# RMS norm of a hybrid decoder step: squared tiles summed on GpSimd, one matmul with ones per norm

## The reference

```
def rmsnorm(x, g, eps=1e-6):
    y = x * lax.rsqrt(jnp.mean(x * x, axis=-1, keepdims=True) + eps)
    return y * g

for i in range(2):
    h = rmsnorm(x, norm_mix[i]);  cp = h @ w_in[i]
    ya, yb, yc = rwkv7(cp...), retention(cp...), mamba2(cp...)
    x = x + concatenate([ya, yb, yc]) @ w_out[i]
    h = rmsnorm(x, norm_ffn[i])
    x = x + (swiglu(h) if i == 0 else moe_swiglu(h))    # top 2 of 8 experts
y = rmsnorm(x, norm_final)
```

## Time and profile before

| | |
|---|---|
| median of three runs | 1709.55 us (1705.39 to 1720.24) |
| the profiled execution, own time | 1713.85 us |
| its span, first to last instruction | 1712.0 us |
| TensorE busy with matmuls | 1522.5 us, 89% of the span, 10644 entries |
| VectorE busy | 926.5 us, 54% |
| ScalarE busy | 741.5 us, 43% |
| GpSimd busy | 110.8 us, 6%, 144 instructions |
| mean granted TensorE clock | 0.853 |

### The profile page before, as it was taken

One profiled execution on the slowest core, in us unless ns is written; L12 is line 12 of the kernel. 1 busy time (PEld: TensorE's weight loads), 2 busy tenths in 40 slices (PEclk: granted clock), 3 DMA queues, 4 the chain that ended last, 5 costly groups with the idle time before them and its releaser, 6 DMA issues.

```text
span 1712.0 us, 27530 instructions
## 1 busy us (share of the span) xinstructions
PE 1522.5 (89%) x10644; PEld 1298.8 (76%) x10644; DVE 926.5 (54%) x1453; ACT 741.5 (43%) x1108; POOL 110.8 (6%) x144
## 2 busy tenths in 40 slices
PE   4899999895889999888999989684899999999996
PEld 3887778773789999877877777473677787778775
DVE  4623544424444344355156533445298888888885
ACT  4511233212343243362113321133187778777874
POOL 0000110201000000000011011100000000000000
PEclk8967888755889999978689985586599999999998
DMA  7211200101534444332120020050197789878982
GB/s 275 89 36 38 68 26 26 53 15 46 183 118 150 137 147 147 123 96 63 38 69 14 26 78 15 42 187 13 38 349 282 285 295 347 283 286 294 348 279 83
DMA packets 62054, 234.83 MB, mean 137 GB/s; under 512 B 7056, under 2 KB 7152, under 8 KB 61072
## 3 DMA queue, kind: packets, MB, share of 16 engines
q1 hardware_dynamic: 59328, 217.61, 37.0%
q0 software_dynamic: 2496, 13.71, 2.1%
q10 hardware_dynamic: 144, 2.28, 0.3%
HBM read 225.48 MB, written 8.09 MB: 136 GB/s over the span
## 4 chain that ended last, share of the span: by engine, by line
PE 55%; issue 31%; DVE 8%; ACT 4%; POOL 1%; DMA 1%; POOLq 0%; ACTq 0%; DVEq 0%
PE bank L459 11%; PE bank L461 9%; PE bank L460 9%; PE bank L453 8%; PE bank L723 2%; ACT whi L1100 2%; PE bank L570 1%; PE bank L473 1%; PE bank L588 1%; PE bank L858 1%; PE bank L602 1%; DVE wlo L1497 1%; PE bank L600 1%; PE bank L811 1%; DMA x<-in_x 1%
## 5 line engine op out<-in xcount | busy, mean ns | idle before, releaser
L1497 DVE TENSOR_TENSOR wlo<-wraw,whi 128x1024 fp32r<-128x1024 f32 x410 | 500.9, 1225 | 406.2 <-ACT whi L1100 393.7
L1100 ACT ACTIVATE whi<-wraw 128x1024 fp32r<-128x1024 f32 x410 | 433.2, 1060 | 442.4 <-PE bank L461 351.4
L459 PE MATMUL bank<-hh,whi 128*128 128x320 f32 x968 | 343.1, 354 | 57.8 <-DVE hl L1517 36.0
L460 PE MATMUL bank<-hl,whi 128*128 128x320 f32 x968 | 318.2, 329 | 0.0
L461 PE MATMUL bank<-hh,wlo 128*128 128x320 f32 x968 | 317.6, 328 | 0.0
L459 PEld LDWEIGHTS bank<-hh,whi 128*128 128x128 f32 x968 | 197.7, 204 | 81.6 <-issue 49.2
L460 PEld LDWEIGHTS bank<-hl,whi 128*128 128x128 f32 x968 | 199.7, 206 | 1.9 <-issue 1.0
L461 PEld LDWEIGHTS bank<-hh,wlo 128*128 128x128 f32 x968 | 199.3, 206 | 0.0
L1018 PE MATMUL bank<-whi,hh 128*128 128x512 f32 (+1 forms) x384 | 148.9, 388 | 1.1 <-DVE place L2043 1.1
L1020 PE MATMUL bank<-wlo,hh 128*128 128x512 f32 (+1 forms) x384 | 144.2, 375 | 0.0
L1019 PE MATMUL bank<-whi,hl 128*128 128x512 f32 (+1 forms) x384 | 144.1, 375 | 0.0
(11 more groups left out here) (380 smaller groups left out, 2205.6 us busy)
## 6 DMA issues: line engine op xcount, KB each, us to landing
wraw<-in_w SPq DMA_DIRECT2D x410, 512.0 KB, 4.9
smb<-in_s_ssm POOLq DMA_DIRECT2D x2, 1536.0 KB, 7.6
out_o_ssm<-smb POOLq DMA_DIRECT2D x2, 1536.0 KB, 5.6
cst<-in_consts ACTq DMA_DIRECT2D x1, 2225.0 KB, 12.6
srw<-in_s_rwkv POOLq DMA_DIRECT2D x2, 768.0 KB, 6.5
out_o_rwkv<-srw POOLq DMA_DIRECT2D x2, 768.0 KB, 4.5
x<-in_x SPq DMA_DIRECT2D x1, 1280.0 KB, 12.4
out_y<-x SPq DMA_DIRECT2D x1, 1280.0 KB, 4.5
```

Source lines behind the costliest of these rows:

```text
L459: mm(out, hi, rh, start=first, stop=False)
L460: mm(out, hi, rl, start=False, stop=False)
L1100: af(whi[:, ring % HI, :], wraw[:, POS[ring], :], ACT.Copy).then_inc(S("slot_hi"), 1)
L1497: tt(wlo[:, POS[ring], :], wraw[:, POS[ring], :], whi[:, ring % HI, :].bitcast(F32), ALU.subtract).then_inc(S("slot_split"), 1)
```

## The change

The squares are no longer multiplied one by one. GpSimd adds the tiles into one (`sums`, new), in the second `htmp` buffer, and TensorE multiplies the ones with that tile alone. A new semaphore `sq_added` says how many tiles are in the sum; it frees the buffers of squares in place of `sq_used`, and `ms_done` lets ScalarE take the root. The first add counts two tiles; each further add waits for the one before, since it reads what that wrote.

```diff
@@ tensor
-            def norm(i, tiles=range(KT)):
-                for k in tiles:
-                    pe.wait_ge(S("sq_ready"), KT * i + k + 1)
-                    m = mm(B[0][:, 0:T], C("ones"), sqb[:, k % 2, :], start=(k == 0), stop=(k == KT - 1))
-                    m.then_inc(S("sq_used"), 1)
+            def norm(i):
+                pe.wait_ge(S("sq_added"), KT * (i + 1))
+                mm(B[0][:, 0:T], C("ones"), htmp[:, 1, :], start=True, stop=True).then_inc(S("ms_done"), 1)
@@ tensor, output projection
                     full_slot(G_OUT[l] + j, G_OUT[l] + j, B[6 + j % 2][:, 0:T])
-                    if j >= 2:
-                        norm(2 * l + 1, [j - 2])
-                norm(2 * l + 1, range(KT - 2, KT))
+                norm(2 * l + 1)
@@ scalar
-                        act.wait_ge(S("sq_used"), KT * i + k - 1)
+                        act.wait_ge(S("sq_added"), KT * i + k - 1)
                     af(sqb[:, k % 2, :], x[:, k, :], ACT.Square).then_inc(S("sq_ready"), 1)
 
             def norm(i):
-                act.wait_ge(S("sq_used"), KT * (i + 1))
+                act.wait_ge(S("ms_done"), i + 1)
@@ gpsimd
+            def sums(i):
+
+                for k in range(1, KT):
+                    gp.wait_ge(S("sq_ready"), KT * i + k + 1)
+                    if k > 1:
+                        gp.wait_ge(S("sq_added"), KT * i + k)
+                    tt(htmp[:, 1, :], sqb[:, 0, :] if k == 1 else htmp[:, 1, :], sqb[:, k % 2, :], ALU.add)\
+                        .then_inc(S("sq_added"), 2 if k == 1 else 1)
...
             gp.dma_start(par[:, :], par_in[0]).then_inc(S("par_in"), 16)
+            sums(0)
             gp.wait_ge(S("const_in"), 16)
             for l in range(DEPTH):
                 if l:
+                    sums(2 * l)
                     gp.wait_ge(S("h_split"), KT * 2 * l + 1)
...
                 out(p_rw[l], srw_p[:, :, :])
+                sums(2 * l + 1)
...
+            sums(2 * DEPTH)
             gp.wait_ge(S("st_out"), 16 * 6 * DEPTH)
```

## The result

The changed kernel takes 1726.06 us (median of 20 runs, 1712.91 to 1739.0), the kernel before 1713.45 us beside it (20 runs, 1698.93 to 1733.9). The ratio is 1.008, interval 1.005 to 1.011: slower by 0.8%, some 12.6 us. The forecast was 2.5 us slower, 1712 on the median of three runs that stood for before then. With 20 runs that base is 1713.45, so of the 14.1 us between 1712 and 1726.06 some 3.9 are the base, and some 10.1 us are missing in the sum. The profiled execution of the changed kernel took 1716.11 us (span 1714.2, mean granted clock 0.850) against 1713.85 (1712.0, 0.853) of before.

What follows compares the result with a forecast made beforehand. TensorE was taken to set the pace in norms 1 and 3, a dependent chain to bound norms 0, 2 and 4. Terms +0.1 - 1.2 + 3.6 - 1.2 + 1.2 gave +2.5 us: 1712 us, range 1704 to 1722.

Steps and rivals of the forecast that it cites:

- Price of one add: GpSimd's chained adds in the norms: 0.93 us a step, with 0.88 and 1.38 as ends.
- rival 1: GpSimd's chained adds: handover costs 0.5 us, not 0.05, step 1.38; slower by 12 us, 1722; chance 13%.
- Contention: Norms 1 and 3: each GpSimd add waits for VectorE's weight split to end, costing nothing within a 3.5 us slot.
- DVE split durations unchanged at 1.23 us: Sign that the forecast is right: VectorE's weight splits keep their length of 1.23 us.
- Rival 3: Norm 0: last add gets no turn until VectorE's three weight splits end; 4.1 us late, 1716; chance 10%.
- The clock: TensorE's single matmuls after over 4 us of idling run at half clock, 1.47 us; restart after the norm loses nothing.
- Norms 1 and 3: Output projections: 2.70 us gained in slots, 1.5 lost at the end; net -1.2 us each, bounds -1.8 and -0.3.
- Norm 2: Bare chain of squares and adds, with nothing to hide it: loss 3.6 us, bounds 2.7 and 6.3.
- Norm 4: Chain of adds longer, but the root's table load becomes hidden: loss 1.2 us, bounds 0.4 and 3.9.
- Norm 0 and the moved DMAs and memsets: Sum arrives just under the weight splits' cover, loss 0.1 us; DMAs and memsets 7.4 us later cost nothing.
- The sum: All five norms together: +0.1 - 1.2 + 3.6 - 1.2 + 1.2 = +2.5 us, 1712 us on the median.
- The bounds: Whole kernel: 1704 to 1722 us, covering all rivals and the scatter of a median; within 1%: 92%.

Runs made afterwards that it cites:

- e5: Changed kernel with three useless ScalarE copies ahead of the root in norms 1 and 3: 1.0156 of before, mean 1729.9 us.
- e8: The kernel before, unaltered, run once more for a second profile: 1717.62 us.
- e1: The changed kernel again, unaltered: 1.0038 (1.0001 to 1.0075) of before, mean 1727.7 us.
- e2: Kernel before with only norms 1 and 3 summed on GpSimd: 0.9928 (0.9882 to 0.9973) of before, mean 1709.0 us.
- e4: Changed kernel with TensorE also multiplying ones with each squared tile in norms 0, 2 and 4, result overwritten: 1.0064 of before, mean 1726.9 us.
- e6: Kernel before with only norms 1 and 3 on GpSimd, repeated on another chip: 0.9948 (0.9893 to 1.0003) of before, mean 1715.9 us.
- e12: Changed kernel with norm 2 alone back on TensorE: 1.0005 (0.9967 to 1.0044) of before, mean 1717.1 us.
- e14: Kernel before with eight useless copies ahead of the root in norm 2, second group: 1.0049 (1.0013 to 1.0085) of before, mean 1726.4 us.
- e7: Kernel before with eight useless copies ahead of the root in norm 2, first group: 1.0117 (1.0046 to 1.0187) of before, mean 1724.0 us.
- e13: Kernel before with four useless copies ahead of the root in norm 2: 1.0004 (0.9974 to 1.0034) of before, mean 1716.9 us.

## Why the prediction was wrong

The direction (slower by less than 1%) and most of the mechanism of the parts were right, the time was not: 1726.06 lies above the range to 1722. The step that failed is the sum. It puts norm 2's longer chain in at its own length, +3.6 us, and everything outside the norms at nothing. Measured, that chain is +3.94 us, but a bare delay of 3.7 us there costs 7.1 and 9.8 us in the means of two groups, the stages behind norms 1 and 3 give +1.7, and the mixers, which had no term, differ by -18.6 and +16.2 us between the two profiles. A further 3.9 us of the distance to 1726 is the base, a median of three executions: on 1713.45 the same sum gives 1716. Point by point:

- **Price of one add.** Forecast 0.93 us a step, measured 1.00 (0.86 for the add). The high end of 1.38, on which rival 1 rested, does not occur; rival 1 would have given 1722, and what came is as slow for another reason.
- **Contention.** As forecast, the add waits for the weight split in norms 1 and 3 and this costs nothing. The Trainium skill, "SBUF — State Buffer", section "Who interferes with whom", says that the first to take the port keeps it; the trace agrees: 1.54 us for the add beside the split, 0.86 alone. In norm 0 it is the other way about: the last add was first, as forecast, and VectorE's split beside it took 1.47 us, against the sign "DVE split durations unchanged at 1.23 us"; nobody waited for it. Rival 3's 4.1 us did not come.
- **The clock.** "The restart after the norm is at half clock already, so nothing is lost there" fails twice. First, the restart is 0.63 and 0.61 us longer, since TensorE works 5.5 and 6.1 us at half clock before the clock rises, instead of 4.1 and 4.8 (20 and 22 matmuls instead of 14 and 17); and SwiGLU has a second such stretch, +1.5 us, against -1.0 in the experts: together +1.7. By e5 this comes with the time of the return, by e8 the SwiGLU part occurs in before too. Second and larger, the clock's course in the mixers is in no term (see the sum below). The matmul priced at 1.47 us took 1.43 or 0.81: half clock after 4.30 us of idling isn't certain, nor is full. Over the twelve norms 1 and 3 in which GpSimd adds (after, e1, e2, e4, e6, e12) it was slow in three and fast in nine, so its price there was mostly too high.
- **Norms 1 and 3.** -1.14 and -1.76, forecast -1.2 each with -1.8 as the end; right. Slots of 3.52 us, right.
- **Norm 2.** +3.94 for a forecast of +3.6, nearly all from the step of 1.00. Right as a stretch, wrong as a price in the sum. A bare delay of 3.7 us in before gives +7.1 us in the mean of one group (e14, 5 either way) and +9.8 in another (e7, 10 either way); undoing norm 2 alone brings the changed kernel back to 1.0005 (e12).
- **Norm 4.** +1.63, forecast +1.2. With TensorE's matmuls this stretch is 8.6 to 10.2 us over seven profiles (mean 9.3), with GpSimd's adds 10.35 to 10.37 over five: +1.1 against that mean, so the forecast is right and the pair's +1.63 partly chance.
- **Norm 0 and the moved DMAs and memsets.** No reader was late. Of the +0.41, 0.23 us is ScalarE's idling ahead of the table load: the cover ends at a step of 0.96 us, as forecast, and the step was 1.00. The rest is less than before's own scatter: norm 0 takes 11.3 to 12.4 us over nine profiles with TensorE's matmuls, since the squares stand 1.07 us apart for more or less of it before they come closer, and 11.9 to 12.0 over seven with GpSimd's adds.
- **The sum.** Fixed stretches +4.8 for a forecast +2.5; of the 2.3 between, 1.7 is the clock behind the norms, and the rest is the step of 1.00 us and the pair's chance in norms 0 and 4, less what norm 3's fast matmul gave. The remaining 5 to 8 us of the measured 10 to 13 were in no term. That they come in the mixer of layer 1, behind norm 2, is argued from e12 and e14 and not measured: that mixer takes 410.9 to 417.6 us in the seven profiles with the long norm 2, 410.2 in e13, and 401.4 to 414.9 in the five with a short one.
- **The bounds.** The forecast took a measurement's scatter of 15 us for noise around a fixed sum. It is not: in every whole kernel measured the times follow the mean granted clock, by 1.3 to 2.1 us for each 0.001, and an edit can change how often the good courses occur.

What is shown: a delay in norm 2, by its length alone, makes before slower (e14, e7), and without norm 2's longer chain the rest of the change costs nothing measurable (e12). What is not: how a delay of 3.7 us keeps the mixer of layer 1 from its short course (401 us in before, 404 in e12, never under 410 with the delay), whether the same delay at another place would do the same (norms 0 and 4 were not tested alone, and e5 leaves it open for norms 1 and 3), and how large the surcharge is. The bare delay costs 7.8 us over e7 and e14 together, 3 to 12, which still holds its own 3.7. That there is more rests on the changed kernel, 9.1 us over its two groups (6 to 12) with fixed stretches of 4.8, and on the 0 of 79 executions. No run holds the clock's course and keeps the delay.

The best version found is the change in norms 1 and 3 alone: 0.993 (0.988 to 0.997) on one chip, 0.995 (0.989 to 1.000) on another, where its mean was not better. Its fixed stretches promise 1.6 us.

## What to carry to other kernels

Matmuls that add up in PSUM get the sum without an instruction of their own. Replacing them by adds pays only where the adds lie beside other work: a chained add of 128x320 costs 1.00 us a step, the square and matmul it replaces 0.71 at full clock (pairs of squares 1.42 us apart in e7), so a norm that nothing covers is longer by all of the difference. At half clock the old pair takes 1.07 us, and adds lose nothing. Norm 4 of e7, where TensorE does the sums (timeline of ScalarE, then the window over it, columns as above, granted clock 0.50):

```profile
1706.92 0.47 ACT L1117 ACTIVATE sqb<-x 128x320 f32<-128x320 f32 x1 [0.60 <-PE bank L473]
1707.98 0.47 ACT L1117 ACTIVATE sqb<-x 128x320 f32<-128x320 f32 x1 [0.60 <-PE bank L473]
1705.00:1710.00 5.00, 5.00 (x11) 2.96 (x10) 0.00 (x0) 1.88 (x4) 0.00 (x0) 0.50 0.01 3
```

Where a profile has long stages with TensorE between its two clocks, look at their granted clock first; a delay of a few us ahead of such a stage may cost twice its length (3.7 us, e14) or nothing that can be measured (1.87 us, e13). One profiled execution of each kernel can't decide there an edit of 1%: here the pair showed +2.3 us for a loss of 10, and only the distribution of some dozens of executions and an undo of one part did.

## What the runs showed of the hardware

The same program, the same 3118 matmuls in each of the mixers whose windows are shown, and mixers of 395.9 to 419.0 us in 26 stages: mean granted clock 0.79 to 0.73 in the four shown above. A single matmul of 128x320 in fp32 behind exactly 4.30 us of idling ran once at full clock in 0.81 us, once at half in 1.43. And a pause of 1.93 us within SwiGLU is followed by half clock in one profile and by full in another. Two windows show it, the changed kernel first, then before, each right behind that pause (columns as above):

```profile
664.50:668.50 4.00, 4.00 (x19) 4.00 (x18) 0.00 (x0) 0.00 (x0) 0.00 (x0) 0.57 0.00 0
```

```profile
683.00:687.00 4.00, 3.90 (x26) 3.91 (x27) 0.04 (x1) 0.97 (x1) 0.00 (x0) 1.00 0.06 24
```

The clock is 0.57 in the first and 1.00 in the second, in the same part of the program. The Trainium skill, "TensorE: Matmul & The Clock Gate", section "What's actually happening", has an idle array drop from 2.4 to 1.2 GHz; the rows agree with the two levels, but the same pause gives either.
